# Split fp32r products for the block's 512-column projections, in a fused two-layer, attention and expert kernel

## What is computed

```python
def second_block(x, c, ctx, ...):
    h = modulate(rms_norm(x, g_attn), sh1, sc1)        # 256 latent tokens
    hc = modulate(rms_norm(ctx, g_attn), csh1, csc1)   # 256 context tokens
    qa, ka, va, qb, kb, vb = split_projection(h @ w_qkv)
    qa_c, ka_c, va_c, qb_c, kb_c, vb_c = split_projection(hc @ w_qkv)
    qa = apply_axial_rope(rms_norm(qa, gqa_q_norm), cos, sin)
    ka = apply_axial_rope(rms_norm(ka, gqa_k_norm), cos, sin); ka_c = rms_norm(ka_c, gqa_k_norm)
    qb = rope_diff(qb, cos, sin); kb = rope_diff(kb, cos, sin)
    mix = concat(gqa_attention(qa, [ka_c, ka], [va_c, va]), diff_attention(qb, [kb_c, kb], [vb_c, vb], lam))
    x = x + gt1 * (mix @ w_o)
    x = x + gt2 * moe_ffn(modulate(rms_norm(x, g_ffn), sh2, sc2), ...)   # 32 experts, 4 per token
    return rms_norm(x, g_final)
```

## Time and profile before

| what | value |
|---|---|
| device time, median of 3 runs | 1963.9 us (1963.8 to 1966.54) |
| device time of the profiled execution | 1962.72 us |
| span in that profile | 1960.9 us |
| PE busy | 1868.4 us, 95% |
| DVE busy | 738.2 us, 38% |
| ACT busy | 574.9 us, 29% |
| POOL busy | 525.4 us, 27% |

### The profile page before, as it was taken

The page is one execution under the profiler, slowest core; times in us unless marked ns, Lnnn a source line. Parts: engine busy times, 40 slices in busy tenths (PEclk is TensorE's granted clock), DMA queues, the critical chain, the costliest instruction groups (busy, mean ns, idle before and its releaser), DMA issues.

```text
span 1960.9 us, 26781 instructions
## 1 busy us (share of the span) xinstructions
PE 1868.4 (95%) x10916; PEld 1179.3 (60%) x10916; DVE 738.2 (38%) x1358; ACT 574.9 (29%) x1042; POOL 525.4 (27%) x220
## 2 busy tenths in 40 slices
PE   7999999989999999999999999999999999999997
PEld 6778889977789899844584444434334443443443
DVE  4776563447855734543543212111111211111112
ACT  4544455444545454323431001101101110110111
POOL 5767656767766557200000000000000000000000
PEclk9999999999999999999989999999999999999999
DMA  8555433555544234621569999999999999999995
GB/s 308 194 193 173 150 108 121 205 178 194 202 172 169 90 130 172 225 87 43 215 266 387 427 428 428 428 428 429 428 428 428 427 427 428 428 429 429 428 428 230
DMA packets 111412, 563.37 MB, mean 287 GB/s; under 512 B 4768, under 2 KB 24352, under 8 KB 86464
## 3 DMA queue, kind: packets, MB, share of 16 engines
q1 hardware_dynamic: 111328, 562.17, 71.6%
HBM read 561.11 MB, written 1.05 MB: 287 GB/s over the span
## 4 chain that ended last, share of the span: by engine, by line
PE 63%; DMA 29%; DVE 5%; ACT 1%; issue 1%; SPq 0%; DVEq 0%; ACTq 0%
DMA ring<-in_e_in_dram 28%; PE bank L1776 15%; PE score L974 11%; PE bank L1766 10%; PE bank L776 5%; PE mixed L1012 4%; PE bank L1743 4%; PE bank L807 2%; PE mixed L1860 1%; DVE ring L2361 1%; PE flip L1843 1%; PE bank L1035 1%; PE score L995 1%; PE score L834 1%; PE mixed L856 1%
## 5 line engine op out<-in xcount | busy, mean ns | idle before, releaser
L2154 POOL TENSOR_TENSOR w_lo<-ring,w_hi 128x1024 fp32r<-128x1024 f32 (+1 forms) x216 | 525.2, 2442 | 271.3 <-ACT w_hi L2053 270.6
L974 PE MATMUL score<-ring,space 128*64 128x512 f32 x2016 | 452.8, 594 | 38.7 <-DMA ring<-in_e_in_dram 37.6
L974 PEld LDWEIGHTS score<-ring,space 128*64 128x64 f32 x2016 | 141.7, 137 | 338.7 <-issue 248.2
L2053 ACT ACTIVATE w_hi<-ring 128x1024 fp32r<-128x1024 f32 (+1 forms) x216 | 226.2, 1049 | 222.7 <-PE bank L1776 113.8
L1776 PE MATMUL bank<-h_hi,w_hi 128*128 128x256 f32 x896 | 260.3, 291 | 0.0
L1776 PE MATMUL bank<-h_lo,w_hi 128*128 128x256 f32 x896 | 252.1, 281 | 0.0
L1776 PE MATMUL bank<-h_hi,w_lo 128*128 128x256 f32 x896 | 251.0, 280 | 0.0
L1012 PE MATMUL mixed<-ring,space 128*64 128x512 f32 x1024 | 226.8, 595 | 0.3 <-ACT space L1243 0.3
L1239 ACT ACTIVATE space<-space 128x512 f32<-128x512 f32 x32 | 20.2, 631 | 696.1 <-DVE space L1549 696.1
L1549 DVE TENSOR_SCALAR space<-score 128x512 f32<-128x512 f32 x32 | 22.2, 693 | 411.5 <-PE score L974 411.5
L1776 PEld LDWEIGHTS bank<-h_hi,w_hi 128*128 128x128 f32 x896 | 168.4, 188 | 4.6 <-issue 4.4
(11 more groups left out here) (348 smaller groups left out, 2307.2 us busy)
## 6 DMA issues: line engine op xcount, KB each, us to landing
ring<-in_e_in_dram SPq DMA_DIRECT2D x126, 2048.0 KB, 25.1
ring<-in_e_out_dram SPq DMA_DIRECT2D x64, 2048.0 KB, 22.1
ring<-in_w_in_dram SPq DMA_DIRECT2D x42, 2048.0 KB, 7.8
ring<-in_w_ada_dram SPq DMA_DIRECT2D x16, 1024.0 KB, 5.2
ring<-in_w_o_dram SPq DMA_DIRECT2D x6, 2048.0 KB, 7.8
ring<-in_w_qkv_dram SPq DMA_DIRECT2D x4, 2048.0 KB, 10.0
ring<-in_w_ada_dram SPq DMA_DIRECT2D x4, 2048.0 KB, 7.9
ring<-in_w_out_a_dram SPq DMA_DIRECT2D x2, 2048.0 KB, 8.3
```

The costliest lines, as they stand in the source:

```text
L974: ins = pe.matmul(score[HALF * blk:HALF * blk + HALF, which * W:(which + 1) * W], xs[:, 2 * j + r, HALF * hh:HALF * hh + HALF], wk[:, blk ...
L2053: act.activation(split_part(w_hi, k), raw_part(k), ACT.Copy).then_inc(hi_done, 1)
L2154: pool.tensor_tensor(split_part(w_lo, k), raw_part(k), split_part(w_hi, k), ALU.subtract).then_inc(lo_done, 1)
```

## The change

The 512-column projections (qa, qb, kb, vb) become split products like those of the layers. The ka units stay 32-bit.

- **Weights.** `split_block` (ACT) rounds a quarter of a raw tile into its high slot; `block_pool` (POOL, new) subtracts and writes the low part over the raw tile. Slots: qa raw and low 5, high 4; qb 1 and 2; kb 0 and 4; vb 5 and 1. That makes 16 roundings and 16 subtractions of 128 x 1024.
- **Activations.** `round_stream` (ACT) rounds `h` and `hc` into slot 3; POOL writes the low parts over `h` and `hc` (as `h_hi` and `context_low`), after the ka units that read them in 32 bits. Two instructions of 128 x 1024 for each stream on each engine.
- **Products.** `project` issues three fp32r products for each 32-bit one and waits for `blo_done` (per quarter) and `low_done` (per half of a stream).
- **Loads.** The qa tile is loaded at the end of layer 2, behind `stream_ready`, and its four roundings stand between the last roundings of the layer. `BLOADS` gives each tile its slot; expert 0's first tiles are loaded in the order 1, 5, 2, 4, 0, 3 (before: 4, 5, 3, 0, 1, 2).
- The buffer `hc` moves to a multiple of 8 words.

POOL goes on into the block with 20 subtractions, in this order. The diff, cut to its core:

```diff
+BLOADS = [("qa", 1, 5), ("ka", 0, 0), ("qb", 2, 1), ("kb", 3, 0), ("vb", 4, 5), ("ada", 7, 2), ("ada", 8, 4),
+          ("out2", 5, 0), ("out2", 6, 3), ("ada", 11, 2), ("ada", 12, 4)]
+BHIGH = {1: 4, 2: 2, 3: 4, 4: 1}
+BSPLIT = [1, 2, 3, 4]
...
+        def split_block(act, i, q):
+            tl = BSPLIT[i]
+            if q == 0:
+                act.wait_ge(landed[BSLOT[tl]], barrived(tl))
+                if tl == 1:
+                    act.wait_ge(stream_ready, LAYERS * 8)
+                elif tl == 2:
+                    act.wait_ge(unit_done, done(LAYERS - 1, NU - 1))
+                else:
+                    act.wait_ge(unit_done, bdone(BLAST[{3: 1, 4: 2}[tl]]))
+            act.activation(high_of(tl)[:, 2 * q:2 * q + 2, :], raw_quarter(i, q), ACT.Copy).then_inc(bhi_done, 1)
...
+            sp.wait_ge(lo_done, split_count(LAYERS - 1, NQ - 1))
+            block_tile(0)
+            block_tile(2)
+            sp.wait_ge(unit_done, bdone(BLAST[0]))
+            block_tile(3)
+            sp.wait_ge(unit_done, bdone(BLAST[1]))
+            block_tile(4)
...
-                    ins = pe.matmul(b[:, 0:n], src[:, c, tt * P:(tt + 1) * P], w8[:, c, 0:n], start=c == 0,
-                                    stop=c == DC - 1)
+                    if c % 2 == 0:
+                        pe.wait_ge(blo_done, 4 * BSPLIT.index(tl) + c // 2 + 1)
+                    if c % 4 == 0:
+                        pe.wait_ge(low_done, 2 * s_ + c // 4 + 1)
+                    x_hi, x_lo, w_h, w_l = stream_high_of[s_], stream_low_of[s_], high_of(tl), low_of(tl)
+                    for x_, w_ in ((x_hi, w_h), (x_hi, w_l), (x_lo, w_h)):
+                        ins = pe.matmul(b[:, :], x_[:, c, cols], w_[:, c, :], start=c == 0 and x_ is x_hi and w_ is w_h,
+                                        stop=c == DC - 1 and x_ is x_lo)
...
+            round_stream(0)
             for u in range(BFIRST - 1):
                 evacuate_block(u)
+                if u < 4:
+                    split_block(act, 1, u)
+                if u == 3:
+                    round_stream(1)
                 if u >= 2:
                     unturn(u - 2)
...
+                if j == 0:
+                    for q in range(4):
+                        split_block(act, 2, q)
+                if j == 2:
+                    for q in range(4):
+                        split_block(act, 3, q)
...
+        def block_pool(pool):
+            def low_tile(i):
+                tl = BSPLIT[i]
+                for q in range(4):
+                    pool.wait_ge(bhi_done, 4 * i + q + 1)
+                    pool.tensor_tensor(low_of(tl)[:, 2 * q:2 * q + 2, :], raw_quarter(i, q),
+                                       high_of(tl)[:, 2 * q:2 * q + 2, :], ALU.subtract).then_inc(blo_done, 1)
+            def low_stream(s_):
+                pool.wait_ge(unit_done, bdone(TT - 1 if s_ == 0 else 2 * TT - 1))
+                for i, piece in enumerate((slice(0, 4), slice(4, 8))):
+                    pool.wait_ge(rounded, 2 * s_ + i + 1)
+                    pool.tensor_tensor(stream_low_of[s_][:, piece, :], (h, hc)[s_][:, piece, :],
+                                       stream_high_of[s_][:, piece, :], ALU.subtract).then_inc(low_done, 1)
+            low_tile(0)
+            low_stream(0)
+            low_tile(1)
+            low_stream(1)
+            low_tile(2)
+            low_tile(3)
...
+                elif debug != "layers":
+                    sp.wait_ge(stream_ready, l * 8 + 8)
+                    sp.dma_start(ring[:, BSLOT[1], :].rearrange("p (c n) -> p c n", c=DC), columns(w_qkv, 0, W)
+                                 ).then_inc(landed[BSLOT[1]], 16)
...
-                split_to(l, NQ)
+                for i in range(4):
+                    split_to(l, NQ - 3 + i)
+                    if l == LAYERS - 1 and debug != "layers":
+                        split_block(act, 0, i)
```

More of the change, by code:

```diff
@@ L256, in build @@
         assert 2 * PARTS * 2 * W + DC * T <= (RING - LRING) * TILE
+        with nc.sbuf_tensor("ring_rounded", [P, MRING, TILE], F32R) as ring_r:
+            pass
         ring = sb("ring", [P, MRING, TILE])
@@ L468, in build @@
         y_ready = sem("y_ready")
-        landed = [sem(f"landed{i}") for i in range(RING)]
+        landed = [sem(f"landed{i}") for i in range(MRING)]
         squared = sem("squared")
@@ L608, in bdone, with barrived, raw_quarter, high_of @@
             return (LAYERS + 1) * NU + u + 1
+        def barrived(tl):
+            slot = BSLOT[tl]
+            order = [t for _, t, s_ in BLOADS if s_ == slot]
+            return (LAYERS * 16 * NT // LRING if slot < LRING else 0) + 16 * (order.index(tl) + 1)
+        def raw_quarter(i, q):
+            return ring[:, BSLOT[BSPLIT[i]], :].rearrange("p (c n) -> p c n", c=DC)[:, 2 * q:2 * q + 2, :]
+        def high_of(tl):
+            return ring_r[:, BHIGH[tl], :].rearrange("p (c n) -> p c n", c=DC)
+        def low_of(tl):
+            return ring_r[:, BSLOT[tl], :].rearrange("p (c n) -> p c n", c=DC)
+        stream_high_of = [ring_r[:, 3, i * DC * T:(i + 1) * DC * T].rearrange("p (c t) -> p c t", t=T)
+                          for i in range(2)]
+        stream_low_of = [h_hi, hc_low]
+        def split_block(act, i, q):
[9 more added lines that the diff above has]
+            act.activation(high_of(tl)[:, 2 * q:2 * q + 2, :], raw_quarter(i, q), ACT.Copy).then_inc(bhi_done, 1)
         def bfreed(u):
@@ L695, in block_sync @@
             sp.dma_start(bin_sb[0:NEXP, :], eb_in).then_inc(bpar_loaded, 16)
-            sp.wait_ge(unit_done, bdone(NBU - 1))
-            for j in (1, 2):
+            for j, last in ((0, BLAST[5]), (3, NBU - 1)):
+                sp.wait_ge(unit_done, bdone(last))
                 expert_tile(e_in[0], e_out[0], j)
@@ L2155, in _ @@
                                        ALU.subtract).then_inc(lo_done, 1)
+            if debug != "layers":
+                block_pool(pool)
         @block.vector
```

76 lines of the change are left out of this document (51 added, 25 removed).

## The result

| kernel | us, median (range, runs) | ratio to the kernel before, 95% interval |
|---|---|---|
| before | 1965.03 (1963.8 to 1966.54, 4) | |
| after | 1980.05 (1978.4 to 1981.55, 4) | 1.0076 [1.0058, 1.0093] |

The change makes the kernel 15.0 us slower. The forecast was +14.3 us, 1978.2 us, and slower with a chance of 0.80; the range was 1965 to 1985.

A forecast was written before the change was run, and what follows sets the result against it. Expert weight loads bound the expert stage, PE sets the pace ahead of it. PE's gain -14.0, waits +3.6, +14.5, +8.9, less 0.7, give +12.3; clock +2 makes +14.3 on 1963.9: 1978.2 us, range 1965 to 1985.

The forecast's parts named there:

- The port: Layers and block: a DVE product of two SBUF tensors, tensor_scalar or copy waits for POOL's running subtraction, up to 2.4 us.
- End of layer 2: Layer end: gained_tables' products get through one per POOL subtraction, so the block starts 3.6 us late.
- ka and qa: Block's first units: PE waits 14.5 us in all before turn(0) to turn(3); scores(0) moves from 839.89 to 855.8.
- The stepping of DVE and ACT: ka and qa units: programs stepped forward, placing unit 0's rotation at 831.9 and unit 3's at 848.5.
- most of it hides in waits: qa halves at the lower clock: mostly hidden in waits for DVE and ACT, only the last halves counting, 0 to 3.4 us.
- the mark that the forecast set as its sign: Profile after: PE idle before turn(0) to turn(3) and turn(5) adding up to 15 us or more.
- the sum: To the end of vb: -14.0 + 3.6 + 14.5 + 8.9 = +13.0, less 0.7 of today's wait, +12.3 us.
- Attention: Attention steps: PE waits 8.9 us, namely turn(5) 4.0, scores(3) 2.0, values(2) 2.7 and scores(1) 0.2.
- The clock: Between 828 and 856 us: PE's granted clock may fall while it waits, costing +2 us in the last halves of qa.
- the rival that it holds through qa and qb: Lower clock paces PE at 5.8 us a half for eight halves: +12 in place of +2, 1988 us, chance 0.07.
- PE's gain: 24 projection halves of qa, qb, kb, vb: 0.56 us each for qa's 4, 0.59 for the other 20, -14.0 us.
- The stream passes the shift on: Expert stage: weights stream at 427 to 429 GB/s without slack, so changes before scores(9) reach the end one for one.

The follow-up runs named there:

- e1: The changed kernel without POOL's 20 subtractions in the block, PE multiplying the high parts three times: 1955.21 us, -7.5 us against the kernel before.
- e5: The changed kernel with all subtractions made but not used, PE waiting for ACT's roundings (low parts only before each tile's last half): 1980.97 us, +15.7 against before.
- e6: The changed kernel with extra unused fp32r products filling PE's waits before turn(0) to turn(3): 1978.70 us, +13.4 us against the kernel before.
- e4: The kernel before with only kb and vb split, subtractions on DVE at idle places, roundings behind the exponentials: 1954.88 us, -7.9 us against before.
- e8: The kernel before with only kb and vb split, roundings behind the exponentials, POOL subtracting as soon as a quarter is rounded: 1969.79 us, +4.5 us.
- e10: kb and vb split with DVE subtracting, plus unused roundings and POOL subtractions of both streams and the qb tile among the ka units: 1970.10 us, +3.6 against before.

## Why the prediction was right, step by step

**The port.** Right, and now shown: e1 against e5 takes away POOL's instructions (and PE's few late waits for them), and 23 us go with them, slow stretches of PE included. The Trainium skill ("SBUF — State Buffer", Who interferes with whom) has a DVE instruction with two SBUF inputs contend with a GpSimd one that reads SBUF, and a copy or tensor_scalar in its 2-port modes fully blocked; the copies that take 4.63 us for two and the 128 x 2 L1451 with 1.08 us agree.

**End of layer 2.** Forecast +3.6; the additions to `x` are 3.6 late, and the first ka product 4.8 (34.01 - 29.23). In e5 and e6 it is 3.7. The rest is the clock: 0.70 in the window at 812 us, where PE sums the squares.

**ka and qa.** The starts of the turns, counted from the first ka product, moved by 3.96, 7.85, 10.76 and 12.69 us. The forecast's waits of 4.2, 4.3, 3.4 and 2.6 less 0.56 for each half between them give 4.2, 7.9, 10.8 and 12.8. The stepping of DVE and ACT was right to 0.3 us. PE's waits themselves were not 14.5 us but 11.1 (3.87, 2.76, 2.03, 2.40): the halves behind `turn(0)` and `turn(1)` ran at the lower clock and filled some 3.3 us of them, which is what "most of it hides in waits" had said. With `turn(5)` PE's waits are 15.0 us, just at the mark that the forecast set as its sign. Then `scores(0)`: +13.6 where 11.6 was forecast. 1.5 of it is the last half of qa, from 854.54 to 858.96, 4.4 us in place of 2.9, at a clock of 0.65. The rest is a slip in the sum: it took off the 0.7 us that PE waits before `scores(0)` as used up, but that wait follows ACT's `unturn` and is still there, 0.69 us. (The 855.8 that the forecast gives for `scores(0)` had kept it: 3.6 + 11.6 on 839.89 would be 855.1.)

**Attention.** `turn(5)` waits 3.93 us (forecast 4.0), `scores(3)` 1.84 (2.0), `values(2)` 2.46 (2.7). From `scores(0)` to `scores(9)` the forecast has -11.8 + 8.9 = -2.9 us; it is 0.0. Two halves at the lower clock are the difference: the last of qb (from 874.60 to `scores(1)` at 879.69, 5.1 us in place of 2.9, window at 0.56), and the one behind `values(2)` (window at 0.50).

**The clock: the term that was mis-sized.** I took +2 us for it, and only in qa (with the rival that it holds through qa and qb). In the profiled execution it costs 1.2 us at the layer's end, 1.5 in qa (`turn(3)` to the next `turn` 4.59 us; 3.65 before, less 0.65), 2.5 in qb (`turn(5)` to `scores(1)` 5.86; 3.96 before, less 0.65) and 2.0 in kb (`scores(3)` to `scores(4)` 14.02; 10.87 before, less 1.3, plus the wait of 2.46): some 7 us. Without it +18.4 would be +11.2. The sum had 12.3, or 13.0 without the slip of 0.7; less 1.2 for PE's gain (20 halves at 0.65 for 0.59) and 0.7 for waits in the attention steps of 8.2 us for 8.9, that is 11.1. Behind `scores(9)` 1.4 us come back, since the kernel before has a slow stretch of its own there. The profiled execution is also the longest of its four. In e5 and e6, whose POOL and ACT work is that of the changed kernel, `scores(9)` comes at +14.9 and +15.3, so there the clock has some 4 us. So over the medians +15.0 stands beside +14.3, but in the profiled execution the clock's term is more than three times what I gave it, and in the two others twice. That the medians agree to 0.7 us is in part luck: the clock was taken too small, PE's gain too small and the waits a little too large. What was wrong in the step is that I looked for slow halves behind the waits of qa alone, not at qb and kb. Why the clock falls behind one wait and not behind another stays open: in e1 it never did before `scores(9)`.

**PE's gain.** Right, and sized a little low: 0.65 us a half in e4, where 0.59 was taken; -10.4 for 16 halves.

**The stream passes the shift on.** Right: -10.4 us at `scores(9)` in e4 is -10.2 at the first expert product, and the medians give -7.9 with their 2.5 us of uncertainty.

## What to carry to other kernels

Before a product is handed to an idle POOL, list what DVE does in that time. In these traces a DVE instruction with two SBUF inputs, a copy or a tensor_scalar on SBUF, even one on two columns, waited for up to the length of one POOL instruction, and again for the next one while POOL ran on. Give such work to DVE itself where it is idle (1.2 us for 2.4, and in e4 nothing was lost), or cut POOL's instructions into short pieces (+0.6 us in place of +15). And split only what the slack covers: all 24 halves with no subtractions at all (e1) gave 7.5 us, no more than 16 halves with all of theirs on DVE (e4, 7.9 us). The 24 halves with DVE subtracting were not run, so how much of the loss that would take back is open.

## What the hardware showed that I had not expected

- POOL pays as well. Its subtraction takes 9.42 / 4 = 2.36 us beside the small products of `gained_tables`, and 10.22 / 4 = 2.56 us beside DVE's rotation of 512 columns, whose products get in between two of POOL's instructions.
- Even an instruction on two columns can wait for nearly the whole of POOL's: L1489 in e8 took 2.24 us in place of 0.17.
- The clock is at its lower level in the work behind a wait: the windows of the changed kernel from 830 to 834 us, where PE waits, show 1.00, and the two behind `turn(0)`, from 835 to 837 us, 0.50. Twelve fp32r products took 4.4 and 5.1 us at two places of one execution, and in e10, where qa is 32-bit, the eight records behind a wait of 4.02 us took 5.94 us in place of 3.60:

```profile
829.80 0.69 PE L877 MATMUL flip<-cst,space 128*128 128x128 f32 x2 [4.02 <-DVEq L1500]
830.28 5.94 PE L857 MATMUL bank<-ring,h 128*128 128x512 f32 x8
...
849.62 3.60 PE L857 MATMUL bank<-ring,h 128*128 128x512 f32 x8
```
